# Rounding the next stage's tiles while the last projection of a stage still runs

## The reference, cut to what matters

```python
mod = (silu(cond) @ mod_w[l] + mod_b[l])
sh1, sc1, g1, sh2, sc2, g2 = split(mod, 6)
h = rmsnorm(x, norm_mix[l]) * (1.0 + sc1) + sh1
if l % 2 == 0:
    q, k, v, g, u, vv = split(h @ ab_w_in[e])
    o_ret, s_f, s_b = retention_bidir(q, k, v, g, ...)      # 4 heads
    o_gm = chunk_gmlp(u, vv, gmlp_ws[e], gmlp_bs[e])        # 4 groups
    mix = concatenate([o_ret, o_gm]) @ ab_w_out[e]
else:
    ...                                                     # RG-LRU
    mix = (gelu(gate_in) * (h_f + flip(h_b))) @ lru_w_out[o]
x = x + g1 * mix
h = rmsnorm(x, norm_mlp[l]) * (1.0 + sc2) + sh2
x = x + g2 * (square(relu(h @ mlp_w1[l])) @ mlp_w2[l])
```

## Time and profile before

| what | us |
|---|---|
| median of 3 runs | 2724.59 |
| lowest and highest | 2723.62, 2724.78 |
| the profiled execution | 2729.32 |
| span of its instructions | 2727.5 |
| granted clock of PE, mean over the span | 0.979 |

### The profile page before, as it was taken

The page is one execution under the profiler, slowest core; times in us unless marked ns, Lnnn a source line. Parts: engine busy times, 40 slices in busy tenths (PEclk is TensorE's granted clock), DMA queues, the critical chain, the costliest instruction groups (busy, mean ns, idle before and its releaser), DMA issues.

```text
span 2727.5 us, 39975 instructions
## 1 busy us (share of the span) xinstructions
PE 2606.4 (96%) x14730; PEld 2519.9 (92%) x14730; DVE 1641.2 (60%) x3056; ACT 666.5 (24%) x1016; POOL 700.0 (26%) x395
## 2 busy tenths in 40 slices
PE   8999999899999999999999889789999999999998
PEld 4999999899999999999998778678999999999998
DVE  5778778548567567567586776865433433343444
ACT  5323323232001001001044545423110110110113
POOL 0211212222222222222223232332223222232221
PEclk9999999999999999999999889899999999999999
DMA  6422222312222222222222101121111111111111
GB/s 229 149 74 68 83 64 74 124 47 64 65 81 69 63 83 69 62 85 69 62 74 104 38 19 38 44 84 39 43 43 39 46 38 46 38 39 46 38 46 70
DMA packets 259139, 181.18 MB, mean 66 GB/s; under 512 B 9205, under 2 KB 253685, under 8 KB 258166
## 3 DMA queue, kind: packets, MB, share of 16 engines
q1 hardware_dynamic: 257924, 169.99, 20.3%
q10 hardware_dynamic: 1138, 10.21, 1.0%
HBM read 165.48 MB, written 14.69 MB: 66 GB/s over the span
## 4 chain that ended last, share of the span: by engine, by line
PE 84%; DVE 10%; issue 3%; ACT 2%; DMA 0%; ACTq 0%; DVEq 0%; POOL 0%; POOLq 0%; SPq 0%
PE psum L588 79%; PE psum L862 2%; DVE mod_sum L1228 2%; DVE work_f L1624 1%; DVE h_lo L1254 1%; DVE sumsq L1197 1%; PE mod_psum L613 1%; DVE x L1275 1%; PE psum L668 1%; DVE sumsq L1260 1%; DVE h_hi L1598 1%; DVE mod_sum L1223 0%; DVE s_bwd L1474 0%; PE psum L743 0%; ACT rate_f L1107 0%
## 5 line engine op out<-in xcount | busy, mean ns | idle before, releaser
L588 PE MATMUL psum<-h_hi,w_hi 128*128 128x384 f32 (+1 forms) x2880 | 678.5, 344 | 37.1 <-DVE h_lo L1254 26.5
L531 POOL CAST w_hi<-w_raw 128x1024 fp32r<-128x1024 f32 x184 | 194.1, 1055 | 1881.6 <-PE psum L588 1028.0
L588 PE MATMUL psum<-h_lo,w_hi 128*128 128x384 f32 (+1 forms) x2880 | 663.1, 339 | 0.0
L588 PE MATMUL psum<-h_hi,w_lo 128*128 128x384 f32 (+1 forms) x2880 | 662.8, 338 | 0.0
L588 PEld LDWEIGHTS psum<-h_hi,w_hi 128*128 128x128 f32 x2880 | 517.9, 190 | 49.2 <-issue 23.1
L1275 DVE SCALAR_TENSOR_TENSOR x<-psum,mod,x 128x768 f32<-128x768 f32 (+2 forms) x432 | 238.5, 610 | 476.4 <-PE psum L588 476.4
L588 PEld LDWEIGHTS psum<-h_lo,w_hi 128*128 128x128 f32 x2880 | 521.9, 190 | 0.0
L588 PEld LDWEIGHTS psum<-h_hi,w_lo 128*128 128x128 f32 x2880 | 521.2, 190 | 0.0
L533 POOL TENSOR_TENSOR w_lo<-w_raw,w_hi 128x1024 fp32r<-128x1024 f32 x184 | 445.3, 2420 | 14.7
L978 ACT ACTIVATE relu<-relu,bias 128x384 f32<-128x384 f32 x128 | 72.0, 610 | 1207.5 <-DVE relu L1326 1207.5
L588 PE MATMUL psum<-hid_hi,w_hi 128*128 128x384 f32 x1536 | 351.9, 336 | 2.8 <-DVE x L1275 2.8
(11 more groups left out here) (223 smaller groups left out, 1888.5 us busy)
## 6 DMA issues: line engine op xcount, KB each, us to landing
w_raw<-in_mlp_w SPq DMA_DIRECT2D x128, 512.0 KB, 4.0
mod_raw<-in_mod_w SPq DMA_DIRECT2D x160, 256.0 KB, 2.9
w_raw<-in_ab_w_in SPq DMA_DIRECT2D x24, 512.0 KB, 4.6
x_spill<-x ACTq DMA_DIRECT2D x2, 4608.0 KB, 13.9
w_raw<-in_lru_w_in SPq DMA_DIRECT2D x16, 512.0 KB, 4.3
x<-x_spill SPq DMA_DIRECT2D x2, 2880.0 KB, 9.3
x_rows<-in_x_sample SPq DMA_DIRECT2D x8, 512.0 KB, 7.6
scale_raw<-in_mod_w SPq DMA_DIRECT2D x8, 512.0 KB, 14.4
```

Of the source, the lines that this page charges most:

```text
L531: pool.tensor_copy(w_hi[:, s, :], w_raw[:, s, :]).then_inc(hi_done, 1)
L588: mm = pe.matmul(psum[:, s, c, 0:end - c * CH], w, v[:, k, c * CH:end], start=(first and n == 0 and w is hi[k] and v is in_hi), stop=(last ...
```

## The change

In the heads: VectorE takes `next_mod(7)` ahead of `unit(5)` in every head. The last head gets code of its own on PE, ScalarE and VectorE. In it, PE counts up `heads_passed` behind each tile of its last projection; ScalarE rounds the six `mix` tiles that are complete as the counts come; VectorE subtracts the first three (`EARLY_DVE`) ahead of `unit(5)`, and GpSimd the next three (up to `EARLY`), between its splits of the first two output units. `out_proj(0)` then only handles tiles 3 and 7.

At both MLPs: PE counts up `out_passed` behind each tile of the last output projection. ScalarE writes `h_hi` from `x` and the gain (`high_direct`) as the counts come, without `gained_out`, and VectorE makes `h_lo` in one step from `x`, gain and `h_hi` (`low_direct`). `updated(7)` comes behind the sixth `low_direct`, and `add_square(7)` behind the eighth.

```diff
@@ three_passes (PE) @@
+                    if free and n < len(tiles) - 1:
+                        mm.then_inc(free, 1)
@@ head (PE) @@
-                big(13, 5).then_inc(unit_done, 1)
+                big(13, 5, heads_passed if isinstance(h, int) and h == HEADS - 1 else None).then_inc(unit_done, 1)
@@ out_proj (PE) @@
-                    project(None, 0, I + c, 0, U + c, width=TOK).then_inc(unit_done, 1)
+                    project(None, 0, I + c, 0, U + c, width=TOK, free=out_passed if c == KT - 1 else None).then_inc(unit_done, 1)
...
-            with pe.Fori(1, HEADS) as h:
+            with pe.Fori(1, HEADS - 1) as h:
                 head(h)
+            head(HEADS - 1)
@@ GpSimd @@
+            def early_low(n):
+                k = MIX_ORDER[0][n]
+                pool.wait_ge(part_hi, H_MIX[0] + n + 1)
+                pool.wait_ge(h_ready, H_MIX[0] + n)
+                pool.tensor_tensor(h_lo[:, k, 0:TOK], mix[:, k, :], h_hi[:, k, 0:TOK].bitcast(F32), ALU.subtract).then_inc(h_ready, 1)
...
+            split(outs, 0)
+            for n in range(EARLY_DVE, EARLY):
+                early_low(n)
+            split(outs, 1)
@@ ScalarE @@
+            def high_direct(n, k):
+                if k == 0:
+                    act.wait_ge(gain_ready, n + 1)
+                for t, c in tokens(x[:, k, :]):
+                    act.activation(h_hi[:, k, c * LAT:c * LAT + t.shape[1]], t, ACT.Copy, scale=gain[:, k, c:c + 1])
+                act.activation(h_hi[:, k, TOK:COLS], mod[:, n // 2, (SH1, SH2)[n % 2] + k, :], ACT.Copy).then_inc(part_hi, 1)
...
                 for k in range(KT - 1):
                     item_out(act, None, 0, AT_OUT[l].items + k)
-                    gain_tile(norm, k)
                     square_tile(norm, k)
-                act.wait_ge(unit_done, AT_MLP[l].units)
                 for k in range(KT):
-                    if k == 4:
+                    if k < KT - 1:
+                        act.wait_ge(out_passed, l * (KT - 1) + k + 1)
+                    else:
                         item_out(act, None, 0, AT_OUT[l].items + KT - 1)
-                        gain_tile(norm, KT - 1)
                         square_tile(norm, KT - 1)
-                    high_part(norm, k)
+                    high_direct(norm, k)
...
+                if last_head:
+                    act.wait_ge(gm_out, HEADS)
+                    for k in MIX_ORDER[0][:EARLY]:
+                        act.wait_ge(heads_passed, k + 1)
+                        mix_part(k)
                 item_out(act, h, HEAD_ITEMS, I0 + 13)
@@ VectorE @@
+            def low_direct(n, k):
+                dve.wait_ge(part_hi, H_NORM[n] + k + 1)
+                for t, c in tokens(x[:, k, :]):
+                    part_of = slice(c * LAT, c * LAT + t.shape[1])
+                    dve.scalar_tensor_tensor(out=h_lo[:, k, part_of], in0=t, scalar=gain[:, k, c:c + 1],
+                                             in1=h_hi[:, k, part_of].bitcast(F32), op0=ALU.mult, op1=ALU.subtract)
+                dve.tensor_tensor(h_lo[:, k, TOK:COLS], mod[:, n // 2, (SH1, SH2)[n % 2] + k, :], h_hi[:, k, TOK:COLS].bitcast(F32),
+                                  ALU.subtract).then_inc(h_ready, 1)
...
                 add_square(norm, KT - 2)
                 for k in range(KT):
-                    low_part(k, gained(norm, k)[:], H_NORM[norm], k)
-                    if k == 1:
+                    low_direct(norm, k)
+                    if k == KT - 3:
                         updated(KT - 1)
-                    if k == KT - 2:
-                        add_square(norm, KT - 1)
+                add_square(norm, KT - 1)
+                if l == 0:
+                    dve.nop().then_inc(gained_ready, KT)
                 reciprocals(norm)
...
                 next_mod(6)
+                next_mod(7)
+                if last_head:
+                    for n in range(EARLY_DVE):
+                        low_part(MIX_ORDER[0][n], mix[:, MIX_ORDER[0][n], :], H_MIX[0], n, TOK)
                 unit(5)
                 s = (I0 + 13) % 2
                 scale_out(s, 5, k_fwd).then_inc(read_out[s], 1)
-                next_mod(7)
                 mini(9)
```

More of the change, by code:

```diff
@@ L313, in build @@
         gate_landed = sem("gate_landed")
+        heads_passed = sem("heads_passed")
+        out_passed = sem("out_passed")
         tanh_ready = sem("tanh_ready")
@@ L343, in col, with first_head @@
             return t[:, n:n + 1] if isinstance(n, int) else t[:, ds(n, 1)]
+        def first_head(h):
+            return isinstance(h, int) and h == 0
         def at(i, per, c):
@@ L553, in _ @@
             split(None, 1)
-            with pool.Fori(1, first) as i:
+            outs = AT_OUT[0].units // 2
+            with pool.Fori(1, outs) as i:
+                split(i, 0)
+                split(i, 1)
+            split(outs, 0)
+            for n in range(EARLY_DVE, EARLY):
+                early_low(n)
+            split(outs, 1)
+            with pool.Fori(outs + 1, first) as i:
                 split(i, 0)
@@ L577, in take_set, with three_passes @@
                 return c % 2
-            def three_passes(s, tiles, hi, lo, in_hi, in_lo, width=TOK, first=True, last=True, before=None, behind=None):
+            def three_passes(s, tiles, hi, lo, in_hi, in_lo, width=TOK, first=True, last=True, before=None, behind=None,
+                             free=None):
                 for n, k in enumerate(tiles):
@@ L598, in parts, with project @@
                 return [view[:, k, start:start + P] for k in range(n)]
-            def project(i, items, item, per, unit, before=None, behind=None, width=COLS):
+            def project(i, items, item, per, unit, before=None, behind=None, width=COLS, free=None):
                 s = take_set(i, items, item)
@@ L604, in project @@
                 return three_passes(s, range(KT), parts(w_hi, unit, KT), parts(w_lo, unit, KT), h_hi, h_lo, width,
-                                    before=before, behind=behind)
+                                    before=before, behind=behind, free=free)
             def mod_column(i, per, c):
@@ L688, in head, with big @@
             def head(h):
-                def big(item, unit):
-                    if not isinstance(h, int) or unit > 0:
-                        return project(h, HEAD_ITEMS, I0 + item, HEAD_UNITS, U0 + unit)
+                def big(item, unit, free=None):
+                    if not first_head(h) or unit > 0:
+                        return project(h, HEAD_ITEMS, I0 + item, HEAD_UNITS, U0 + unit, free=free)
                     tile_ready, sum_squares = norm_waits(0)
@@ L1030, in _, with head @@
             I0, U0, M0 = AT_MIX[0].items, AT_MIX[0].units, AT_MIX[0].minis
-            with act.Fori(0, HEADS) as h:
-                steps.enter(h, 9)
+            def head(h, last_head):
+                steps.enter(None if last_head else h, 9)
                 def mini(n):
@@ L1083, in _ @@
                 act.activation(by_bank(tile_of(mix, h)), whole(s), ACT.Copy).then_inc(read_out[s], 1)
-            steps.leave(HEADS)
+                steps.leave(1 if last_head else HEADS - 1)
+            with act.Fori(0, HEADS - 1) as h:
+                head(h, False)
+            head(HEADS - 1, True)
             out_proj(0)
@@ L1281, in out_proj @@
                 if l == 0:
-                    for n, k in enumerate(MIX_ORDER[l]):
-                        low_part(k, mix[:, k, :], H_MIX[l], n, TOK)
+                    dve.wait_ge(h_ready, H_MIX[l] + EARLY)
+                    for n in range(EARLY, KT):
+                        low_part(MIX_ORDER[l][n], mix[:, MIX_ORDER[l][n], :], H_MIX[l], n, TOK)
                 else:
@@ L1402, in _, with head @@
             I0, U0, M0 = AT_MIX[0].items, AT_MIX[0].units, AT_MIX[0].minis
-            with dve.Fori(0, HEADS) as h:
-                steps.enter(h, 41 + 14 * HEAD_MODS)
+            def head(h, last_head):
+                steps.enter(None if last_head else h, 41 + 14 * HEAD_MODS)
                 def unit(n):
@@ L1541, in _ @@
                 mods_out(0, h * HEAD_MODS + FIRST_MODS, HEAD_MODS, at(h, HEAD_MODS, FIRST_MODS + HEAD_MODS))
-            steps.leave(HEADS)
+                steps.leave(1 if last_head else HEADS - 1)
+            with dve.Fori(0, HEADS - 1) as h:
+                head(h, False)
+            head(HEADS - 1, True)
             out_proj(0)
```

30 lines of the change are left out of this document (15 added, 15 removed).

## The result

| | median us | lowest to highest | runs |
|---|---|---|---|
| before | 2724.78 | 2722.31 to 2732.47 | 7 |
| after | 2734.35 | 2733.22 to 2735.63 | 7 |

The ratio is 1.0028 (1.0018 to 1.0037). That is slower by 9.6 us between the medians and by 7.6 us (4.9 to 10.1) by the ratio; 2733.2 us was predicted. The profiled execution after took 2733.53 us (span 2731.7). Lines have moved in the file: L771 is now L793, L613 is L635, L588 is L608, L1270 is L1321, L1228 is L1269, L1254 is L1295, the column sums of the squares (L635) are L657.

A forecast was written before the change was run, and what follows sets the result against it. TensorE (PE), busy 96% of the span, was taken as the bound, so only its waits or lower clock matter. 9.6 + 0.4 - 1.4 = +8.6 us on the 2724.59 us median gave 2733.2 us; range 2725 to 2740.

The forecast's parts named there:

- Part 1: Ends of heads 0 to 2: modulation sum ahead of unit 5's eviction starts each next head 3.2 us later, +9.6 us.
- The same 1.7 as lost: Ends of heads 0 to 2: the low clock around PE's wait still loses 1.7 us each, so no change.
- swap hidden: Rival, heads' ends: PE's wait only changes its place; the other parts alone give 2723.6 us; chance 0.08.
- a second slow stretch: Rival, every head's end: another stretch at low clock, +1.7 us x 3, 2738.3 us; chance 0.14.
- Part 2: End of the last head: removed wait replaced by PE's delayed last product, output projection starts +0.4 us (-1.5 to +2).
- as low again: End of the last head: clock, 0.57 over 491 to 503 before, assumed low after the change too.
- Part 3: Start of both MLPs behind output projections: last square 2.4 us earlier, 1.7 lost to clock; -0.7 each, -1.4 us.
- the seams give nothing: Rival, both MLP starts: last square's add, longer tiles and clock eat the early start; +10.2 us, 2735; chance 0.10.
- the clock kept: Rival, both MLP starts: gathered wait doesn't lower the clock, 2 x 1.7 us come back; +5.2, 2729.8 us; chance 0.14.

## Why the prediction was right, step by step

**Part 1** held in its mechanism and in its size: +3.2 us at each of three heads, measured 3.14 to 3.24. It came otherwise than foretold, though: the next head's first matmul is 4.6 to 5.0 us later, not 3, and 1.5 to 1.7 come back inside that head. Item 15 follows the eviction by 0.05 us, the one wait is 5.14 to 5.21 us (some 5.2 was said), and tile 7's fetch is late as worked out: its sum ends 5.46 us behind tile 6's, where 5.3 was taken. "The same 1.7 as lost" held as a sum, at another place: 4.21 us of item 15 at heads 1 and 2 instead of 2.24, against 1.5 to 1.7 that the big matmuls have back. The rival "swap hidden" falls by these rows. So does the price of "a second slow stretch": the low stretch did become twice as long, but PE stands for 40 to 50% of it. The proof outside the profile is the 10.3 us (8.4 by the ratios) between the changed kernel and the one with the swap in the last head alone. What the step did not see is a second cost of the old order: where GpSimd's split starts early (5.1 and 5.2 us behind unit 5 instead of 5.5 to 5.8), it catches the sum's last steps, and a head's end takes 9.7 to 9.8 us (one head in each of three experiments' profiles; in two of them another takes 7.5 to 7.6). With the swap in heads 0 to 2 no step of the sum there is over 0.35 us in any of the three profiles. That this is why the changed kernel's runs lie within 2.4 us of each other isn't shown: with the square added early, and the same swap, they spread over 9.0.

**Part 2** had its sum about right (-0.2 for +0.4) by luck, from two terms that were both off and nearly cancel. Item 15 at the lower clock, 4.21 us instead of the 2.25 taken from the earlier trace rows, makes the start 2.15 us later, not 0.4; and the clock, taken "as low again" over the output projection, is not low there, which gives 2.32 back. One slow stretch stood in the wrong place in the sum. Nor did it ask why PE waits 5.08 us here before and 2.10 at head 0: the rest is GpSimd's split over the sum.

**Part 3** was mis-sized: -0.3 for -1.4. At seam B the last add ends 14.46 us behind the output projection, where it was 16.52: 2.06 earlier, not 2.4, as GpSimd's split held two low parts by 2.9 us (0.79 and 2.15 over 1.54), not 2.3. A low part costs 1.55 as taken. The slow clock cost 1.83 at B and 2.03 at C, not 1.7. The rival "the seams give nothing" came nearest here. That with the clock kept falls: at seam C the windows have 0.72 over 1900 to 1912, where the earlier trace rows have 1.00 and the waits of before came as 2.74, 1.57 and 1.00 us. Seam C was not the whole of before, though: at seam B waits of 2.74 and 1.31 us had the clock low as well, while PE was waiting for VectorE anyway:

```profile
604.00:612.00 8.00, 6.69 (x25) 6.08 (x24) 6.83 (x7) 4.70 (x7) 1.22 (x1) 0.57 0.22 66
```

So waits in pieces did not by themselves keep the clock. The section "HAM oscillation — how this bites in real kernels" of the Trainium skill (TensorE: Matmul & The Clock Gate), by which long waits between bursts make each burst start cold, agrees with the wait of 5.09 us here, and with its absence in the run with the early square (1.00 over 1880 to 1900 and over 612 to 624).

The three parts measured make +9.1, where +8.6 was forecast. The first carries it; that the errors of the second (-0.6) and the third (+1.1) partly cancel is luck, and 2.3 us at the RG-LRU gates stand in no part.

## What to carry to other kernels

Before moving work ahead of a wait, look for what the moved-past instruction releases: here an eviction freed the accumulators that the bottleneck engine's next product needed, and a sum of 4.4 us put in front of it cost 3.2 net, three times. An edit that takes waits away is worth only what it takes from the last of them: six tiles without a wait gave at most 0.2 us a seam, and one add moved up by two places, with its update, 6.8 to 7.0. And an engine that is "free" to help isn't free if its instructions stand beside a chain of another that is on the path: gate the help behind that chain.

## What the runs showed of the hardware

While GpSimd works on tiles in SBUF, VectorE's instructions with two inputs there stand: one step took 2.50 us instead of 0.35 beside a subtraction of 2.34, fourteen took 11.55 instead of 4.0 beside the last two of three low parts (8.28 in all) and a split. Of these fourteen it was four that stood, for 2.72, 2.69, 1.12 and 2.50 us; the other ten took some 0.35 each. A step with one tile input stood too (1.61 us instead of 0.28, the first of the two at 490.44). GpSimd can be the one that stands: in the run with its low parts taken away its cast took 2.27 us instead of 1.04 beside the steps of the sum. Evictions out of PSUM aren't held: the one at 278.13 of the changed kernel began 0.3 us into a cast of GpSimd's and took 1.35 us, as at 169.84. Nor were the 124 evictions into `relu` that began within an instruction of GpSimd's: 0.55 us by the median, like the 68 others. The Trainium skill, SBUF — State Buffer, section "Who interferes with whom", has it that the two share a read port that is locked for a whole instruction, so that the order of issue decides who stands; the rows agree, and add the price to a chain of short instructions: each may lose a whole one of GpSimd's.

The slow stretch of the clock is charged to whatever PE does behind its wait. With a small product there, that one paid (4.21 us for 2.24) in place of the big ones.
